# Turning the sample state on VectorE and by copies inside SBUF instead of on TensorE, in a hybrid mLSTM and gated-MLP layer

## The reference

```python
h = rmsnorm(x);  proj = h @ w_in            # q, k, v, o, za, gates, u, vb, zb, ga, gb
qk, conv_new = causal_conv(concat(q, k), conv_state)     # width 4, per channel; conv_new: last 3 rows
# branch A, 8 heads of 256; C is value x key, one 256x256 state a head and sequence
num = (s * wts) @ v + sc_inter * einsum('bhvk,bthk->bthv', C, q)
den = sum(s * wts)   + sc_inter * einsum('bhk,bthk->bth', n, q)
C_new = decay * C + einsum('bsh,bshv,bshk->bhvk', ws, v, k)
y_a = sigmoid(o) * rmsnorm_head(num / max(|den|, exp(-m))) * silu(za)
# branch B
y_b = u * (tril(w_s) @ layernorm(vb) + b_s) * silu(zb)
merged = sigmoid(ga) * (y_a @ w_pa) + sigmoid(gb) * (y_b @ w_pb)
y = x + rmsnorm(merged @ w_out)
```

## Time and profile before

| | |
|---|---|
| time, median of 3 runs | 1530.59 us (1530.47 to 1530.62) |
| the profiled execution | 1530.92 us, its span 1529.4 us |
| TensorE busy | 1509.9 us, 99% of the span |
| VectorE busy | 892.9 us, 58% |
| ScalarE busy | 660.0 us, 43% |
| GpSimd busy | 91.6 us, 6% |
| moved by DMA | 268.03 MB, mean 175 GB/s |

### The profile page before, as it was taken

How to read it: one execution, slowest core, us unless ns; L and a number is a source line. 1 busy time by engine, 2 the same in 40 slices (tenths; PEclk the granted TensorE clock), 3 DMA queues, 4 the chain that set the end, 5 groups by cost and what they waited for, 6 DMA issues and landing times.

```text
span 1529.4 us, 30905 instructions
## 1 busy us (share of the span) xinstructions
PE 1509.9 (99%) x11419; PEld 1502.4 (98%) x11419; DVE 892.9 (58%) x1533; ACT 660.0 (43%) x932; POOL 91.6 (6%) x171
## 2 busy tenths in 40 slices
PE   9999999999999999999999999999999999999996
PEld 9999999999999999999999999999999999999996
DVE  7755565654444457666766666666766644444444
ACT  6433433433333344454545454545444433333442
POOL 4000000001000000101010101001010000000000
PEclk9999999999999999999999999999999999999998
DMA  7664555556555544564637373737474545555543
GB/s 233 204 171 152 162 168 159 148 180 221 165 165 165 165 151 141 180 199 153 227 121 259 113 267 112 266 114 254 126 243 136 189 162 167 162 166 186 172 153 136
DMA packets 234049, 268.03 MB, mean 175 GB/s; under 512 B 9152, under 2 KB 222728, under 8 KB 233152
## 3 DMA queue, kind: packets, MB, share of 16 engines
q1 hardware_dynamic: 221360, 226.26, 47.2%
q0 software_dynamic: 12400, 41.23, 7.7%
q10 hardware_dynamic: 256, 0.10, 0.0%
HBM read 244.48 MB, written 23.06 MB: 175 GB/s over the span
## 4 chain that ended last, share of the span: by engine, by line
PE 92%; issue 6%; DVE 1%; ACT 1%; DMA 0%; POOL 0%; DVEq 0%; ACTq 0%; POOLq 0%
PE ps L395 27%; PE ps L396 27%; PE ps L397 27%; PE ps L571 2%; PE ps L559 2%; PE ps L583 1%; PE ps L703 1%; PE ps L630 1%; PE ps L528 1%; DVE otok L1518 0%; DMA xt<-in_x_prompt_dram 0%; PE ps L668 0%; PE ps L404 0%; ACT hb L772 0%; PE ps L429 0%
## 5 line engine op out<-in xcount | busy, mean ns | idle before, releaser
L1010 DVE TENSOR_TENSOR wlo<-raw,whi 128x1024 fp32r<-128x1024 f32 x416 | 508.0, 1224 | 553.8 <-ACT whi L755 552.2
L395 PE MATMUL ps<-xh,whi 128*128 128x288 f32 x2560 | 765.3, 299 | 0.0
L755 ACT ACTIVATE whi<-raw 128x1024 fp32r<-128x1024 f32 x416 | 441.0, 1061 | 741.8 <-PE ps L397 724.4
L397 PE MATMUL ps<-xh,wlo 128*128 128x288 f32 x2560 | 755.3, 295 | 0.0
L396 PE MATMUL ps<-xl,whi 128*128 128x288 f32 x2560 | 754.6, 295 | 0.0
L395 PEld LDWEIGHTS ps<-xh,whi 128*128 128x128 f32 x2560 | 481.1, 188 | 0.3
L396 PEld LDWEIGHTS ps<-xl,whi 128*128 128x128 f32 x2560 | 480.7, 188 | 0.2
L397 PEld LDWEIGHTS ps<-xh,wlo 128*128 128x128 f32 x2560 | 480.6, 188 | 0.0
L396 PE MATMUL ps<-yl,whi 128*128 128x288 f32 x512 | 151.5, 296 | 0.0
L395 PE MATMUL ps<-yh,whi 128*128 128x288 f32 x512 | 150.8, 294 | 0.0
L397 PE MATMUL ps<-yh,wlo 128*128 128x288 f32 x512 | 150.6, 294 | 0.0
(11 more groups left out here) (326 smaller groups left out, 1199.5 us busy)
## 6 DMA issues: line engine op xcount, KB each, us to landing
raw<-in_w_in_dram SPq DMA_DIRECT2D x320, 512.0 KB, 3.5
raw<-in_w_pb_dram SPq DMA_DIRECT2D x32, 512.0 KB, 3.3
Cin<-in_state_mlstm_C_dram POOLq DMA_DIRECT2D x16, 1024.0 KB, 8.7
out_dram<-Cin POOLq DMA_DIRECT2D x16, 1024.0 KB, 6.2
raw<-in_w_pa_dram SPq DMA_DIRECT2D x32, 512.0 KB, 3.3
raw<-in_w_out_dram SPq DMA_DIRECT2D x32, 512.0 KB, 3.3
out_dram<-cpo POOLq DMA_DIRECT2D x8, 256.0 KB, 2.4
xres<-in_x_prompt_dram SPq DMA_DIRECT2D x1, 2048.0 KB, 8.4
```

The costliest lines, as they stand in the source:

```text
L395: nc.tensor.matmul(out, whi[:, c, kk, cols], mh_[:, k, :], start=(k == 0), stop=False)
L397: last = nc.tensor.matmul(out, wlo[:, c, kk, cols], mh_[:, k, :], start=False, stop=(k == KT - 1))
L755: nc.scalar.activation(whi[:, c], raw[:, c], ACT.Copy).then_inc(hi_ready, 1)
L1010: nc.vector.tensor_tensor(wlo[:, c], raw[:, c], whi[:, c].bitcast(F32), ALU.subtract).then_inc(lo_ready, 1)
```

## The change

- **C is turned without TensorE.** VectorE transposes each 32x32 block of `Cin` in place in the grid (`turn_blocks(h, b)`, two instructions of 128x256 for a sequence) into `Xb`, which holds four sequences. SP then moves the blocks to their partitions with 16 copies from SBUF to SBUF for each four sequences (`move_blocks`), from 32 partitions to 32 partitions each, into `Yb`. `turn_blocks` runs behind the splits of K2 and K3 (b = 0 to 3), behind V3 (4, 5) and O0 (6, 7). SP's copies stand in its list behind the loads of V0 to V3 and O0 to O3, four behind each, and the first of each sixteen waits for the turned blocks. `Xb` is free for b = 4 when the first sixteen have landed.
- ScalarE rounds from `Yb` instead of PSUM to `CTh`; VectorE puts the rest back in place in `Yb`; both parts of n stand in two columns beside `CTh`, so the low product has 256 columns for 258, and the two parts of the denominator are added later.
- **`part` goes to DRAM.** It holds one pair of blocks; Pool stores it after each pair of MB and loads it for each of MA. VectorE waits for the buffer (`part_free`) before it writes it, and for the last store before the fills at the head stage's start.
- **The conv rows are turned on VectorE**, by one 128x128 instruction of 32x32 blocks each way. The rows then stand in four groups of partitions, so that Pool loads them by 8 transfers for 4, and stores them by 16 for 2. TensorE's wait for `bcrow` moves from behind Q1 to behind Q2.
- Pool stores and loads the first half of C ahead of C_p and the second half.

The diff, cut to its core:

```diff
 sp:
+        def move_blocks(h, half_, g):
+            if g == 0:
+                sp.wait_ge(xb_set, 8 * h + 4 * half_ + 4)
+                sp.nop(nofuse=True)
+            rows = slice(32 * g, 32 * g + 32)
+            for to in range(4):
+                sp.dma_start(Yb[32 * to:32 * to + 32, :, g, 4 * half_:4 * half_ + 4, :],
+                             Xb[rows].rearrange("p (k g) b r -> p k g b r", g=4)[:, :, to]).then_inc(y_in[half_], 16)
         def load_pair(...):
                 sp.dma_start(raw[:, c], w[c, :, :, ds(col, PW)]).then_inc(raw_landed[c], 16)
+                if after is not None:
+                    move_blocks(*after, c)
...
-                load_pair(H0 + j + 5 * h, w_in_v, col + PW * h)
+                load_pair(H0 + j + 5 * h, w_in_v, col + PW * h, after=(h, j - 2) if j in (2, 3) else None)
 pe:
-        def c_turn(h, b):
...
             for kh in range(2):
-                for part_ in (CTh, CTl):
-                    last = nc.tensor.matmul(ps[:, X4, 0:DH + 2], qm[...], part_[:, kh, :], ...)
+                nc.tensor.matmul(ps[:, X4, 0:DH + 2], qm[...], CTh[:, kh, :], ...)
+                last = nc.tensor.matmul(ps[:, X4, 0:DH], qm[...], of_c(b)[:, kh].bitcast(F32R), ...)
...
-                if c == 1:
-                    pe.wait_ge(hst_in, 64 * h + 64)
+                if c == 2:
                     pe.wait_ge(bc_row, h + 1)
-                    pe.transpose(ps[:, X4, 0:P], hst[:], ident[:]).then_inc(hist_t, 1)
...
-                    for b in range(4):
-                        last = pe.transpose(ps[0:27, X5, P * b:P * b + P], cn[:, b, :], ident[:])
 act:
         def ct_copy(h, b):
-            act.wait_ge(ct_t, 8 * h + b + 1)
-            nc.scalar.activation(key_major(CTh), turned(b), ACT.Copy).then_inc(ct_ev, 1)
+            if b % 4 == 0:
+                act.wait_ge(y_in[b // 4], 256 * h + 256)
+            if b > 0:
+                act.wait_ge(inter_mm, 8 * h + b)
+            nc.scalar.activation(by_group(CTh), of_c(b), ACT.Copy).then_inc(ct_ev, 1)
 dve:
+            dve.wait_ge(part_free, i + 1)
-            nc.vector.scalar_tensor_tensor(part[:, ds(2 * i, 2), :], tg[:], 1.0, ...)
+            nc.vector.scalar_tensor_tensor(part[:], tg[:], 1.0, ...)
...
+        dve.wait_ge(part_free, 9)
         nc.vector.memset(hb[:], 0.0)
...
+        def turn_blocks(h, b):
+            if b % 4 == 0:
+                dve.wait_ge(c_in[b // 4], 16 * h + 16)
+            if b == 4:
+                dve.wait_ge(y_in[0], 256 * h + 256)
+            for vh in range(2):
+                last = nc.vector.transpose(Xb[:, :, b % 4, vh::2], Cin[:, b, vh, :])
+            last.then_inc(xb_set, 1)
...
                 split_lo(H0 + 1 + 5 * h, c)
                 if c == 1:
+                    dve.wait_ge(hst_in, 128 * h + 128)
+                    nc.vector.transpose(hT[:]..., hst[:]...).then_inc(hist_t, 1)
...
+                if c >= 2:
+                    for b in (2 * c - 4, 2 * c - 3):
+                        turn_blocks(h, b)
...
                 split_lo(H0 + 2 + 5 * h, c)
                 if c == 3:
                     last.then_inc(qm_set, 1)
+                    for b in (4, 5):
+                        turn_blocks(h, b)
...
                 split_lo(H0 + 3 + 5 * h, c)
                 ct_split(h, c)
                 if c == 0:
+                    for b in (6, 7):
+                        turn_blocks(h, b)
...
+                    nc.vector.transpose(cst[:]..., cn[:]...).then_inc(cst_ev, 1)
...
+            dve.wait_ge(part_in, 16 * i + 16)
-            nc.vector.tensor_tensor(sm[:], tm[:], part[:, ds(2 * i, 2), :], ALU.add).then_inc(ma_sum, 1)
+            nc.vector.tensor_tensor(sm[:], tm[:], part[:], ALU.add).then_inc(ma_sum, 1)
 pool:
+            pool.dma_start(part_d[ds(i, 1)].squeeze(0), part[:]...).then_inc(part_out, 16)
+            pool.wait_ge(part_out, 16 * i + 16)
+            pool.sem_inc(part_free, 1)
...
+            for g in range(0, P, S):
+                for s in range(2):
+                    pool.dma_start(blocks_of(conv_p_v, h, s, g), cst[g:g + 3, 2 * s:2 * s + 2, :]).then_inc(cst_out, 16)
+                    pool.dma_start(blocks_of(conv_s_v, h, s, g), cst[g + 3:g + 27, 2 * s:2 * s + 2, :]
+                                   ).then_inc(cst_out, 16)
```

More of the change, by code:

```diff
@@ L192, in build @@
     a = Area(phase)
-    part = a("part", [P, KT, T])
+    part = a("part", [P, 2, T])
+    part_d = nc.dram_tensor("part_d", (8, P, 2 * T), F32)
+    a = Area(phase)
+    Xb = a("Xb", [P, 8, 4, 64])
     after_part = a.at
@@ L325, in x_bank, with of_c, by_group @@
         return 2 + k % 6
[L328 to L332, removed]
+    def of_c(b):
+        return Yb[:, :, :, b, :]
+    def by_group(t):
+        return t[:, :, 0:DH].rearrange("p k (g r) -> p k g r", g=4)
     @block.sync
@@ L340, in _, with load_pair @@
         sp.dma_start(xt[:, 1, HALVES[1]], xp_v[:, 1, HALVES[1]]).then_inc(x_in_rest, 16)
-        def load_pair(pair, w, col, first=False):
+        def move_blocks(h, half_, g):
[6 more added lines that the diff above has]
+                             Xb[rows].rearrange("p (k g) b r -> p k g b r", g=4)[:, :, to]).then_inc(y_in[half_], 16)
+        def load_pair(pair, w, col, first=False, after=None):
             for c in range(CHUNKS):
@@ L569, in inter @@
             for kh in range(2):
-                for part_ in (CTh, CTl):
[L571 to L574, removed]
+                nc.tensor.matmul(ps[:, X4, 0:DH + 2], qm[:, kh, 2 * S * b:2 * S * b + P], CTh[:, kh, :],
+                                 start=(b == 0 and kh == 0), stop=False, skip_group_check=True)
+                last = nc.tensor.matmul(ps[:, X4, 0:DH], qm[:, kh, 2 * S * b:2 * S * b + P],
+                                        of_c(b)[:, kh].bitcast(F32R), start=False,
+                                        stop=(b == NB - 1 and kh == 1), skip_group_check=True)
             last.then_inc(inter_mm, 1)
@@ L1312, in _ @@
                 if c == 1:
+                    dve.wait_ge(hst_in, 128 * h + 128)
+                    nc.vector.transpose(hT[:].rearrange("p j r -> p (j r)"),
+                                        hst[:].rearrange("p j r -> p (j r)")).then_inc(hist_t, 1)
                     dve.wait_ge(hist_t, h + 1)
@@ L1423, in _ @@
                     dve.wait_ge(num_mm, h + 1)
-                    for t, (n, bank) in enumerate(((P, 6), (P, 7), (S, 4))):
-                        last = nc.vector.tensor_copy(f3[0:n, t:t + 1], ps[0:n, bank, DH:DH + 1])
+                    for t in range(2):
+                        nc.vector.tensor_copy(f3[:, t:t + 1], ps[:, 6 + t, DH:DH + 1])
+                    last = nc.vector.tensor_reduce(f3[0:S, 2:3], ps[0:S, 4, DH:DH + 2], mybir.AxisListType.X, ALU.add)
                     den = Steps(dve, den_step, 3 * h)
@@ L1602, in load_c, with blocks_of @@
                            Cs_in[:, 4 * half_:4 * half_ + 4, ds(h, 1)].rearrange("p b o n -> p (b o) n")).then_inc(c_in[half_], 16)
+        def blocks_of(rows, h, s, g):
+            return rows[:, s, ds(DH * h, DH)].rearrange("r (a f) -> r a f", a=2)[:, :, g:g + S]
         def load_hist(h):
-            for b in range(4):
-                pool.dma_start(hst[S * b:S * b + HIST * NB, :], conv_in_v[:, b // 2, ds(DH * h + P * (b % 2), P)]
-                               ).then_inc(hst_in, 16)
+            for g in range(0, P, S):
+                for s in range(2):
+                    pool.dma_start(hst[g:g + HIST * NB, 2 * s:2 * s + 2, :], blocks_of(conv_in_v, h, s, g)
+                                   ).then_inc(hst_in, 16)
+        pool.sem_inc(part_free, 1)
         pool.wait_ge(yg_lo, GROUPS)
@@ L1615, in _ @@
         load_hist(0)
+        with pool.Fori(0, 8) as i:
+            pool.wait_ge(slot_free[1], MB_USE[1] + 1 + i)
+            pool.nop(nofuse=True)
+            pool.dma_start(part_d[ds(i, 1)].squeeze(0), part[:].rearrange("p j t -> p (j t)")).then_inc(part_out, 16)
+            pool.wait_ge(part_out, 16 * i + 16)
+            pool.sem_inc(part_free, 1)
         def h_body(h, more=True):
@@ L1619, in h_body @@
             pool.nop(nofuse=True)
-            for rows, out in ((slice(0, 3), conv_p_v), (slice(3, 27), conv_s_v)):
-                pool.dma_start(out[:, :, ds(DH * h, DH)], cst[rows].rearrange("r (s a) b -> r s (a b)", s=2)
-                               ).then_inc(cst_out, 16)
+            for g in range(0, P, S):
+                for s in range(2):
+                    pool.dma_start(blocks_of(conv_p_v, h, s, g), cst[g:g + 3, 2 * s:2 * s + 2, :]).then_inc(cst_out, 16)
+                    pool.dma_start(blocks_of(conv_s_v, h, s, g), cst[g + 3:g + 27, 2 * s:2 * s + 2, :]
+                                   ).then_inc(cst_out, 16)
             if more:
@@ L1647, in _, with load_part @@
         h_body(HEADS - 1, more=False)
+        def load_part(i):
+            pool.dma_start(part[:].rearrange("p j t -> p (j t)"), part_d[ds(i, 1)].squeeze(0)).then_inc(part_in, 16)
```

(5 more changed lines are left out.)

94 lines of the change are left out of this document (47 added, 47 removed).

## The result

The changed kernel takes 1618.76 us, median of 4 runs (1617.61 to 1619.01), against 1530.55 for the kernel before beside it: ratio 1.0574, 95% interval 1.0561 to 1.0587. The profiled execution took 1618.74 us with a span of 1617.2. It is slower by 88.2 us, where 51 were forecast.

The account below looks back on a forecast made before the run. TensorE, busy 80.93 of 81 us in the second head, was taken as the bound. Stalls 2.7 + 6.35 less 4.07 saved, eight heads 39.8, less 1.6, gave 1569.1; clock 12.8 made 1582 us, range 1558 to 1608, over all 1545 to 1620.

Parts of the forecast that it names:

- What goes from TensorE: Transposes of Cin, cn and hst leave TensorE, 4.07 us a head, 32.6 in all; its 1.6 us bcrow wait goes too.
- What is hidden: Part's other stores and loads, Pool's small conv transfers and C's stores and loads delay nothing; Pool's transfers have 4 us cover.
- The turn's price: On VectorE, a 128x256 block turn takes 0.35 us; four turns, for two sequences, take 1.4 us.
- the rival of the slow turn: VectorE's turns cost 0.69 us each, adding 5.4 us a head: 1612.6 us, with the clock 1625; chance 0.14.
- First and second stall: TensorE waits for the CT subtraction ahead of inter(h,0), 2.7 us, and inter(h,1), 6.35 us, in each head.
- A copy's issue on SP: Each copy takes 0.45 us to issue in SP's queue, four 1.8 us; bounds 0.37 and 0.62.
- The copy's extra landing: Copies on SP's queue add nothing to the next load's landing; bounds 0 and 1 us.
- The clock: TensorE's granted clock falls to half once a head, at the second stall, costing 1.6 us a head, 12.8 in all.
- the rival of the full-chunk clock with both stalls: TensorE's clock costs a full chunk a head, 1594.5 us; if the first stall drops it too, 1620; chance 0.15.
- V1 is what the first stall waits for: V1's load, late behind SP's copies, sets the 2.7 us first stall; rival without that: stall 0.4, 1551 us, chance 0.10.
- The gain stands: Rival: loads of V1 and O1 are issued by SP in time, so the run takes 1496.7 us; chance 0.08.

Follow-up runs that it names:

- the filler: Changed kernel plus matrix products nobody reads on TensorE, 18 ahead of a head's first product with C and 30 ahead of its second: 1605.77 us.

## Why the prediction came out as it did

The sign and the mechanism were right; the time was 37 us too low. The measured 1618.8 lies outside the forecast's own 1558 to 1608. It lies within 1545 to 1620 by 1.2 us, close to an end that rivals set whose prices did not come true, and that is luck. By its own steps:

- **What goes from TensorE**, 32.6 + 1.6 us: right as far as it could be tested. The wait for bcrow is gone, and the parts without C gave 7.9 where 6.0 were priced. C's 3.52 us a head were not measured alone. With the filler, the 1605.8 are 1522.7 and the stalls of 107.5 to 110.5 less what C's turning gave back: that leaves 24.4 to 27.4 us for it, 3.1 to 3.4 a head.
- **What is hidden**: right. The 16 stores of cn's rows and the 8 loads of hst end on Pool at 715.6, the power operation comes at 731.96, VectorE never waits for it. With C's turning back on TensorE all of this costs nothing.
- **The turn's price**: right. Four turns are 1.42 us busy, 1.34 to the next instruction's start; 1.4 was taken. The estimate of 0.62 for one, by doubling the width, is refuted: the 128x256 turn took 0.41 us and the 128x128 turn of hst 0.30, so twice the width was far from twice the price. That sinks the rival of the slow turn, although its 1612.6 to 1625 holds the measured time.
- **First and second stall**: this is the step that failed, in size. At full clock they are 13.4 to 13.8 us a head, 9.05 were forecast; 8 x 4.3 to 4.7 = 35 to 38 us is the whole miss. Two terms carry it, what four copies and a load cost SP and how long that load takes to arrive; the rest of the chain was right to within half a microsecond. In the second head the stalls are 12.9 us; the first head's first one is longer, some 7.7. The second distance, subtraction to subtraction, is 695.27 - 683.67 = 11.6 us against 10.0: the turn 1.34 (1.4 taken), four copies and the start of the load 688.08 - 685.08 = 3.0 (1.8), issue to ScalarE's start 4.2 (3.5), from there to the subtraction's end 2.99 (3.07), SP's wake 0.07 (0.2). In the first chain V1 arrives 7.37 us behind the turns (5.5 taken), V2 3.40 behind V1 (2.25); from V2's arrival to SiLU 2.38 (2.4). That chain is 3.0 us longer than forecast by V2's arrival, and 2.1 to 2.3 of it reach the stall (2.7 forecast, 4.8 to 4.9 measured).
- **A copy's issue on SP**, 0.45 taken with bounds 0.37 and 0.62: the median is 0.597 busy, starts 0.64 apart, and a load behind four of them follows 0.3 us later still. I chose by SP's loads; Pool's issue, the other bound, was nearer. **The copy's extra landing**, 0 taken, bound 1: the load behind copies took 4.2 and 4.4 us from its issue to ScalarE's start.
- **The clock**, 1.6 a head: right in what it adds, 13.0 us for 12.8. But the picture was wrong: both stalls bring the clock down, not the second alone. TensorE's time between its waits is some 4.7 us a head longer ((88.2 + 1.6 + 32.6 - 84.6) / 8), of which only 1.6 reach the end: a slow stretch behind the first stall delays TensorE toward a second one in which it would have waited. That is why the second recorded stall is 5.2 us and not 8.0. The rival of the full-chunk clock with both stalls gives 1620, next to the measured 1618.8, for a reason that the kernel with filler refutes: without any clock loss the time is still 1605.8.
- **V1 is what the first stall waits for**: right against its rival; with V1 to V3 ahead of the copies ScalarE's waits for raw go from 191.1 to 14.0 us. But the load that ends last there is V2, as in the forecast's own chain: it arrives at 674.46, and behind it stand ScalarE's table load and the SiLU, which starts at 676.84, while the convolution behind V1 has ended at 675.19.
- **The gain stands**, 1496.7: no kernel here reached it. The best with the whole change, 1525.3, is 5.4 us faster than before. It is 28.6 above 1496.7, and TensorE's recorded waits in it are 22.0 us (26.5 for its weight loads). Whether its late first load comes from the load on the DMA engines or from SP's wait was not separated. The version without the C part, 1522.7, is the fastest that was run.

## What to carry over

When copies join an ordered DMA queue, price the load behind them: issue times add up one after the other, and a semaphore wait in that queue makes every later load as late as the engine it waits for. Price a stall from full clock and keep the clock as a second term that may be swallowed by the next stall; a filler that ends inside the stall measures it. When one wait is removed, look for the next on the same chain (here SP's wait, then the one buffer Xb, then VectorE's order) before counting the gain.

## What the runs showed of the hardware

- An SBUF-to-SBUF copy of 64 KB kept SP's queue 0.60 us, against 0.39 for a load of 512 KB; on Pool's queue it was 0.54. So the smaller transfer was the dearer one to issue. These copies landed after 2.9 us (median), and after 4.3 to 5.1 when two queues carried them. That the second queue makes the difference is not shown: with a quarter of the copies, on SP alone, each between two loads, it was 4.6.
- The granted clock fell within TensorE's stalls, 0.69 from 682 to 683 and 0.81 from 692 to 693, stayed at 0.50 (1.2 GHz) while it worked again, from 684 to 689 and up to 699, and came back as it went on working, 1.00 from 700 to 702. In the kernel with a quarter of the copies it was 0.50 behind a stall of 1.8 us too. With filler in the stalls it was 0.997 over the span, at stalls as long.
- A 32x32-block turn of 128x256 float32 took 0.406 us (median) and 0.34 to the next, one of 128x128 0.30 us. Elementwise operations of 128x256 took 0.29 us (the kv copy) and 0.35 (a masked product in the changed kernel).
